# Gate/up with the activations stationary and 512 moving weight columns, x turned before it is normalised, two layers unrolled

## What is computed

```python
D_MODEL, SEQ, DEPTH, D_FF = 1024, 256, 2, 2816

def rms_norm(x, g):
    y = x * rsqrt(mean(x * x, -1) + 1e-6)
    return y * g

def swiglu_ffn(x, w_gate, w_up, w_down):
    return (silu(x @ w_gate) * (x @ w_up)) @ w_down

x = x + 0.5 * swiglu_ffn(rms_norm(x, ffn_norm), w_gate, w_up, w_down)
```

## Time and profile before

| | |
|---|---|
| median of 3 runs | 1089.12 us (1088.06 to 1089.48) |
| profiled execution, from its first to its last instruction | 1087.3 us; it is the time of that execution that the profile gives |
| TensorE busy | 1053.6 us (97%) |
| VectorE busy | 587.2 us (54%) |
| ScalarE busy | 493.3 us (45%) |
| GpSimd busy | 103.5 us (10%) |
| mean rate from memory | 164 GB/s |

### The profile page before, as it was taken

One profiled execution on the slowest core, in us unless ns is written; L12 is line 12 of the kernel. 1 busy time (PEld: TensorE's weight loads), 2 busy tenths in 40 slices (PEclk: granted clock), 3 DMA queues, 4 the chain that ended last, 5 costly groups with the idle time before them and its releaser, 6 DMA issues.

```text
span 1087.3 us, 18211 instructions
## 1 busy us (share of the span) xinstructions
PE 1053.6 (97%) x7148; PEld 949.8 (87%) x7148; DVE 587.2 (54%) x630; ACT 493.3 (45%) x656; POOL 103.5 (10%) x165
## 2 busy tenths in 40 slices
PE   6999999999989999999989999999998999999996
PEld 6999999778768999999889999998796789999995
DVE  4644454755665654445465544457456655445544
ACT  6443344447434544443364344335555354433342
POOL 2000000330341000000010000005004210000000
PEclk9999999999979999999999999999999899999999
DMA  9565455253212455545545555554252126554551
GB/s 327 197 219 186 182 190 193 80 192 140 106 56 88 158 191 193 193 169 182 191 166 197 191 193 187 181 173 148 99 181 78 39 79 232 187 183 174 190 204 48
DMA packets 26277, 178.38 MB, mean 164 GB/s; under 512 B 3152, under 2 KB 3664, under 8 KB 5360
## 3 DMA queue, kind: packets, MB, share of 16 engines
q1 hardware_dynamic: 24912, 174.73, 44.3%
q0 software_dynamic: 880, 2.74, 0.8%
q10 hardware_dynamic: 432, 0.18, 0.1%
HBM read 176.94 MB, written 1.05 MB: 164 GB/s over the span
## 4 chain that ended last, share of the span: by engine, by line
PE 63%; issue 28%; POOL 5%; ACT 1%; DVE 1%; DMA 1%; POOLq 0%; DVEq 0%; SPq 0%; ACTq 0%
PE psum L882 20%; PE psum L883 20%; PE psum L884 20%; POOL mixer_scratch L306 3%; PE psum L1103 1%; PE psum L899 1%; DMA w_raw<-in_w_dram 1%; PE psum L972 1%; ACT w_high L367 1%; POOL statistics L283 1%; POOL mixer_scratch L333 0%; POOL mixer_scratch L338 0%; POOL statistics L293 0%; ACT mixer_scratch L438 0%; PE psum L967 0%
## 5 line engine op out<-in xcount | busy, mean ns | idle before, releaser
L588 DVE TENSOR_TENSOR w_low<-w_raw,w_high 128x2048 fp32r<-128x2048 f32 x163 | 375.3, 2305 | 245.7 <-ACT w_high L367 245.7
L882 PE MATMUL psum<-xT_high,w_high 128*128 128x256 f32 x1536 | 436.1, 284 | 5.4 <-DVE xT_low L593 4.5
L883 PE MATMUL psum<-xT_low,w_high 128*128 128x256 f32 x1536 | 434.6, 283 | 0.0
L884 PE MATMUL psum<-xT_high,w_low 128*128 128x256 f32 x1536 | 434.6, 283 | 0.0
L367 ACT ACTIVATE w_high<-w_raw 128x2048 fp32r<-128x2048 f32 x163 | 311.1, 1914 | 124.9 <-PE psum L884 119.9
L882 PEld LDWEIGHTS psum<-xT_high,w_high 128*128 128x128 f32 x1536 | 294.6, 192 | 8.9 <-DVE xT_low L593 5.3
L883 PEld LDWEIGHTS psum<-xT_low,w_high 128*128 128x128 f32 x1536 | 294.6, 192 | 1.5
L884 PEld LDWEIGHTS psum<-xT_high,w_low 128*128 128x128 f32 x1536 | 294.6, 192 | 0.0
L396 ACT ACTIVATE silu_gate<-psum 128x256 f32<-128x256 f32 x88 | 33.7, 383 | 273.1 <-PE psum L884 273.1
L882 PE MATMUL psum<-w_high,hT_high 128*128 128x512 f32 (+1 forms) x360 | 139.9, 389 | 0.0
L883 PE MATMUL psum<-w_low,hT_high 128*128 128x512 f32 (+1 forms) x360 | 139.7, 388 | 0.0
(11 more groups left out here) (163 smaller groups left out, 804.9 us busy)
## 6 DMA issues: line engine op xcount, KB each, us to landing
w_raw<-in_w_dram SPq DMA_DIRECT2D x163, 1024.0 KB, 4.8
x<-in_x_dram SPq DMA_DIRECT2D x2, 512.0 KB, 4.3
mixer_scratch<-in_fil_dram POOLq DMA_DIRECT2D x2, 512.0 KB, 6.8
out_dram<-x_normed SPq DMA_DIRECT2D x4, 256.0 KB, 2.1
mixer_scratch<-in_fil_dram POOLq DMA_DIRECT2D x2, 384.0 KB, 7.4
mixer_scratch<-in_fil_dram POOLq DMA_DIRECT2D x2, 352.0 KB, 5.9
dft<-in_dft_dram SPq DMA_DIRECT2D x1, 512.0 KB, 6.8
inverse_dft<-in_dft_dram SPq DMA_DIRECT2D x1, 512.0 KB, 6.5
```

Source lines behind the costliest of these rows:

```text
L588: e.tensor_tensor(WL[p][:], raw[p][:], WH[p][:].bitcast(F32), ALU.subtract).then_inc(s_lo.sem, 1)
L882: e.matmul(out, ah, bh, start=start, stop=False)
L883: e.matmul(out, ah, bl, start=False, stop=False)
L884: return e.matmul(out, al, bh, start=False, stop=stop)
```

## The change

It does these things:

- Gate/up has x stationary and the weights moving. A slot now holds four of the eight inner tiles with 256 gate and 256 up columns side by side, so each of 48 matmuls per chunk has 512 moving columns. The product is tokens x hidden units: one PSUM bank per token tile (4 and 5), no second set.
- Since down needs hidden units x tokens, TensorE transposes the 128 x 128 blocks of `hidden` in float32 (`turn_hidden`, four per chunk, into bank 6), and `ht_high` and `ht_low` read that bank.
- Before an FFN x is transposed as it is (`turn_x`), partly between the last matmuls of the stage before; rstd enters as the scale of silu and as a factor in `gate`. Before the mixer, VectorE writes x times rstd (`normed`), and TensorE transposes that. No diagonal, no product with it.
- GpSimd multiplies rstd by sqrt(1024) in a fourth step.
- The loop over the layers is unrolled; linked waits are on constants. The spare fetch at the end goes.
- At stage ends two slots' splits, not one, are made before the updates.

```diff
+XT_BANKS = [(7, 6), (0, 1)]
+HT_BANK = 6
...
-            def x_rstd(l, j, link=link):
+            def x_rstd(l, j):
...
-                    e.tensor_tensor(r, r, cst[:, I_POW:I_POW + 1], ALU.pow).then_inc(s_rstd.sem, 1)
+                    link(e.tensor_tensor(r, r, cst[:, I_POW:I_POW + 1], ALU.pow))
+                    e.tensor_tensor(r, r, cst[:, I_SD:I_SD + 1], ALU.mult).then_inc(s_rstd.sem, 1)
...
+            def x_high(l, turn, t, half, col):
+
+                g = 2 * t + half
+                e.wait_ge(s_tr.sem, s_tr.at(l, 4 * turn + g + 1))
+                for n in range(4):
+                    k = 4 * half + n
+                    r = e.activation(XH[:, k, t * P:(t + 1) * P], PS[:, XT_BANKS[t][half], n * P:(n + 1) * P], ACT.Copy,
+                                     scale=par[:, col + k:col + k + 1])
+                r.then_inc(s_xh.sem, 1)
+
+            def enter(l, j, turn, col):
+
+                e.wait_ge(s_par.sem, s_par.at(l))
+                x_high(l, turn, 0, 0, col)
+                x_high(l, turn, 0, 1, col)
+                squares(l, j, (0,))
+                x_high(l, turn, 1, 0, col)
+                x_high(l, turn, 1, 1, col)
+                squares(l, j, (1,))
...
+                e.activation(sg[:, t, :], PS[:, 4 + t, 0:SEQ], ACT.Silu, scale=st[:, T_R + t:T_R + t + 1]).then_inc(s_silu.sem, 1)
...
+            def ffn(l, f, base, j, turn, col, after):
+                if l or f:
+                    enter(l, j, turn, col)
+                for t in range(T):
+                    e.wait_ge(s_rstd.sem, s_rstd.at(l, 2 * j + t + 1))
+                hi(l, base + 2)
+                hi(l, base + 3)
+                for t in range(T):
+                    silu(l, j, f * CH, t, base + 1)
+                ht_high(l, f * CH, 0, 0)
+                hi(l, base + 4)
 
                 def chunk(c, pr):
 
+                    q = f * CH + c
+                    ht_high(l, q - 1, 1, 1 - pr)
+                    hi(l, base + 3 * c + 2, (pos(base + 2), base // RING + c + 1))
+                    for t in range(T):
+                        silu(l, j, q, t, base + 3 * c)
+                    ht_high(l, q, 0, pr)
+                    hi(l, base + 3 * c + 3, (pos(base), base // RING + c + 2))
+                    hi(l, base + 3 * c + 4, (pos(base + 1), base // RING + c + 2))
...
-            squares(0, 0)
-            hi(0, 0)
             e.wait_ge(s_par0.sem, 16)
             e.sem_inc(s_par.sem, 1)
-            with e.Fori(0, DEPTH) as l:
+            enter(0, 0, 0, C_G1)
+            hi(0, 0)
+            hi(0, 1)
+            for l in range(DEPTH):
...
+            def normed(l, j, t):
 
                 e.wait_ge(s_rstd.sem, s_rstd.at(l, 2 * j + t + 1))
+                e.tensor_scalar(xn[:, t, :], x[:, t, :], st[:, T_R + t:T_R + t + 1], None, ALU.mult).then_inc(s_xn.sem, 1)
...
+            def gate(l, q, t):
+                e.wait_ge(s_silu.sem, s_silu.at(l, 2 * q + t + 1))
+                e.scalar_tensor_tensor(out=hid[:, t, :], in0=PS[:, 4 + t, SEQ:2 * SEQ], scalar=st[:, T_R + t:T_R + t + 1], in1=sg[:, t, :],
+                                       op0=ALU.mult, op1=ALU.mult).then_inc(s_h.sem, 1)
...
+            def update_and_enter(l, slot, scale, j, at, turn, col):
+
+                update(l, slot, scale, j, 0, 0)
+                update(l, slot, scale, j, 0, 1)
+                x_low(at, turn, 0, 0, col)
+                update(l, slot, scale, j, 1, 0)
+                x_low(at, turn, 0, 1, col)
+                update(l, slot, scale, j, 1, 1)
+                x_low(at, turn, 1, 0, col)
+                x_low(at, turn, 1, 1, col)
...
+            def ffn(l, f, base, after):
+                lo(l, base + 2)
+                lo(l, base + 3)
+                for t in range(T):
+                    gate(l, f * CH, t)
+                ht_low(l, f * CH, 0, 0)
+                lo(l, base + 4)
                 if f == 0:
                     argument(l, 0, 7, C_FB1, C_FF1)
...
+                    ht_low(l, q - 1, 1, 1 - pr)
+                    lo(l, base + 3 * c + 2, pos(base + 2))
+                    for t in range(T):
+                        gate(l, q, t)
+                    ht_low(l, q, 0, pr)
+                    lo(l, base + 3 * c + 3, pos(base))
+                    lo(l, base + 3 * c + 4, pos(base + 1))
...
                 lo(l, FFN2)
-                update(l, S_WO + 3, 1.0, 1)
-                ffn(l, 1, FFN2, 2, 3, C_G2)
+                lo(l, FFN2 + 1)
+                update_and_enter(l, S_WO + 3, 1.0, 1, l, 3, C_G2)
...
+            def turn_x(l, j, t, half):
+
+                e.wait_ge(s_x.sem, s_x.at(l, 4 * j + 2 * t + half + 1))
+                for n in range(4):
+                    k = 4 * half + n
+                    r = e.transpose(PS[:, XT_BANKS[t][half], n * P:(n + 1) * P], x[:, t, k * P:(k + 1) * P], ident)
+                r.then_inc(s_tr.sem, 1)
...
+            def gate_up(l, turn, n, p, half, tiles, fresh=False):
+
+                for t in tiles:
+                    for kk in range(4):
+                        k = half * 4 + kk
+                        if fresh and kk == 0:
+                            e.wait_ge(s_xl.sem, s_xl.at(l, 4 * turn + 2 * t + half + 1))
+                        r = passes(PS[:, 4 + t, :], XH[:, k, t * P:(t + 1) * P], XL[:, k, t * P:(t + 1) * P], WH[p][:, kk, :], WL[p][:, kk, :],
+                                   k == 0, k == KD - 1)
+                    if half and t == 0:
+                        r.then_inc(s_gu.sem, 1)
+                    if t == 1:
+                        r.then_inc(s_used.sem, 1)
+
+            def turn_hidden(l, q, t):
+
+                e.wait_ge(s_h.sem, s_h.at(l, 2 * q + t + 1))
+                for h in range(2):
+                    r = e.transpose(PS[:, HT_BANK, h * SEQ + t * P:h * SEQ + (t + 1) * P], hid[:, t, h * P:(h + 1) * P], ident)
+                r.then_inc(s_ht.sem, 1)
...
+                e.wait_ge(s_lo.sem, s_lo.at(l, base + 1))
+                gate_up(l, turn, base, pos(base), 0, (0,), True)
+                if l or f:
+                    turn_x(l, j, 1, 0)
+                    turn_x(l, j, 1, 1)
+                e.wait_ge(s_lo.sem, s_lo.at(l, base + 2))
+                gate_up(l, turn, base + 1, pos(base + 1), 1, (0,), True)
+                gate_up(l, turn, base, pos(base), 0, (1,), True)
+                gate_up(l, turn, base + 1, pos(base + 1), 1, (1,), True)
+                if f == 0:
+                    filter_mm(l, 0, F_W1, fil[:, F_Z:F_Z + SEQ], HYE, 7)
+                turn_hidden(l, f * CH, 0)
...
+                    e.wait_ge(s_lo.sem, s_lo.at(l, base + 3 * c))
+                    e.wait_ge(s_h.sem, s_h.at(l, 2 * q))
+                    gate_up(l, turn, base + 3 * c - 1, pos(base + 2), 0, range(T))
+                    e.wait_ge(s_hl.sem, s_hl.at(l, 2 * q - 1))
+                    turn_hidden(l, q - 1, 1)
+                    e.wait_ge(s_lo.sem, s_lo.at(l, base + 3 * c + 1))
+                    gate_up(l, turn, base + 3 * c, pos(base), 1, range(T))
+                    e.wait_ge(s_hl.sem, s_hl.at(l, 2 * q))
+                    turn_hidden(l, q, 0)
...
+                    down(l, base + 3 * c + 1, pos(base + 1), q - 1, 1 - pr, first)
```

More of the change, by code:

```diff
@@ L659, in ffn @@
                     chunk(i * 2 + 3, 1)
-                chunk(CH - 1, (CH - 1) % 2)
                 q, pr = f * CH + CH - 1, (CH - 1) % 2
-                gate(l, q, 0, pr)
+                ht_low(l, q - 1, 1, 1 - pr)
                 lo(l, base + FFN_SLOTS - 1)
+                for t in range(T):
+                    gate(l, q, t)
                 ht_low(l, q, 0, pr)
-                gate(l, q, 1, pr)
+                if after is not None:
+                    lo(l, after)
                 ht_low(l, q, 1, pr)
@@ L1064, in project @@
                 return r
-            with e.Fori(0, DEPTH) as l:
-                ffn(l, 0, 0, 0, 0)
+            e.wait_ge(s_cst.sem, 16)
+            for t in range(T):
+                turn_x(0, 0, t, 0)
+                turn_x(0, 0, t, 1)
+            for l in range(DEPTH):
+                ffn(l, 0, 0, 0, 0, None)
                 e.wait_ge(s_in.sem, 16 * N_IN)
@@ L1235, in ffn_slots @@
         at = slice(c * 256, (c + 1) * 256)
+        both = np.concatenate([gate[:, at], up[:, at]], 1).reshape(2, 4, P, 512)
         for half in range(2):
-            r = slice(at.start + half * P, at.start + (half + 1) * P)
-            a = np.stack([gate[:, r].reshape(KD, P, P), up[:, r].reshape(KD, P, P)], 2)
-            out.append(a.transpose(1, 0, 2, 3).reshape(P, SLOT))
+            out.append(both[half].transpose(1, 0, 2).reshape(P, SLOT))
         if last is not None:
```

319 lines of the change are left out of this document (154 added, 165 removed).

## The result

The changed kernel takes **1103.18 us** (1101.95 to 1105.51, 4 runs) against 1089.03: **1.0135** times the time before, 95% interval 1.0122 to 1.0148. It is slower, where 1092.7 (1079 to 1100) was forecast. The profiled execution took 1102.18, its span is 1100.3 us, 13.0 more than before.

The account below looks back on a forecast made before the run. TensorE, busy 1053.6 of 1087.3 us, was taken as the bound: its instructions' start-to-start distances plus gaps between stages. Terms summed to +3.6, 1087.3 to 1090.9 in span, forecast as 1092.7 us, range 1079 to 1100.

Parts of the forecast that it names:

- The clock: Half-clock falls behind new TensorE idles: 0 to 10 us; two places of 3.8 us idle counted, +4.
- Steady chunks: Gate/up in chunks 1 to 10 of four FFNs: wide matmuls gain 0.60, transposes take 0.44; 0.16 per chunk, 6.4 us less.
- The knife edge: Each steady chunk: new `hidden` is ready 0.1 us before its transposes; 0 taken, 0.3 per chunk (12 us) as bad end.
- Rival 3: Steady chunks: `hidden` late by 0.15 us in 40 chunks adds 6, giving 1099 us; chance 0.16.
- Rival 4: Gate/up: a wide matmul costs as much as two narrow steps, adding 26 us, giving 1119; chance 0.03.
- FFN 2's entry: Entry to FFN 2: gate/up starts 3.0 us earlier, but TensorE idles 3.8 before chunk 1; +0.8 each, +1.6.
- rival 1: Stage entries: `hidden` of chunk 0 ready when gate/up ends, so idles and clock falls go; 1081 us, chance 0.17.
- FFN 1 to mixer: Entry to the mixer, twice: x updates begin later behind a second w_low; 1.4 us later each, +2.8.
- Layer edge: Between the layers, once: jump and table load go, but updates wait for two w_low; -1.3 us.
- Start: Kernel start: ScalarE's x copies and squares precede the weight split, gate/up at 18.7 us, chunk 1 at 32.2; +4.5.
- Tail and unrolling: Output stored earlier at the end, -1.9 us; register instructions before linked waits go, mostly in the mixer, -0.6.
- Rival 2: Mixer keeps its clock because shorter POOL and VectorE links close the waits; 11 us less, 1082, chance 0.11.

Follow-up runs that it names:

- experiment 1: Changed kernel with filler transposes of the identity into a free bank in TensorE's idle places (start, mixer entries, before chunk 1); 1092.63 us, ratio 1.0025.
- narrow: Changed kernel with each gate/up matmul of 512 moving columns split into two of 256; 1126.53 us.
- twice_turned: Changed kernel with every pair of transposes of `hidden` issued twice into the same place; 1122.45 us.
- experiment 6: The run `narrow`: changed kernel with each gate/up matmul of 512 moving columns split into two of 256; 1126.53 us.
- experiment 9: Changed kernel with start, gate and updates reordered, tile-by-tile waits and the third slot's copy moved up; 1082.77 us, ratio 0.9930.
- experiment 4: Kernel before the change with only its loop over the two layers unrolled on every engine; 1085.48 us, ratio 0.9975.
- experiment 11: Kernel before the change with its layers unrolled and filler transposes in three waits of the mixer; 1082.84 us, ratio 0.9946.
- experiment 2: Changed kernel with the start reordered: squares first, then each x tile's copies alternating with a weight slot's; 1104.35 us, ratio 1.0129.
- combo2: The run of experiment 9: changed kernel with start, gate and updates reordered, tile-by-tile waits and the third slot's copy moved up; 1082.77 us, ratio 0.9930.
- combo3_fill: `combo2` plus filler (start, mixer), filter fetch ahead of the edge's rstd, both tiles multiplied with the first weight slot first; 1067.22 us, ratio 0.9807.
- experiment 5: Changed kernel with the second early w_low of each stage end put back behind the x updates; 1094.11 us, ratio 1.0043.
- experiment 3: Changed kernel with silu and gate product of chunk 0 ahead of the fourth slot's split, in all FFNs; 1095.49 us, ratio 1.0051.

## Why the prediction was wrong

The span came out 9.4 us above the forecast's 1090.9, and the range ended 3 us short. The queues were forecast rightly. The step that failed is the count of the clock's falls, which makes 3.1 of the 9.4. The others: some 2 in the chunks, 1.4 at the start, about 1 at the two mixer entries, and 0.9 because layer 2's mixer spent 13.7 us at half level and not 10.2, which is luck.

- **The clock: the step that failed.** "I count the two places of 3.8 us, +4." The same paragraph lists idles of 2.9 (twice) and 2.6, and at the start TensorE stands still for 10 us; none of these was counted. In the profiled execution all came: six stretches, not two. Filled, the six gave back 7.1 us (experiment 1), 3.1 more than the +4. The two that were counted cost 1.6 and 1.5 where 2 each was taken. The upper end of 10 us was in the text, but with it the sum is 1098.7, past the forecast's own 1096 and just inside the range; no room was left for the sum's other errors.
- **Steady chunks: right mechanism, too small a price.** -6.4 was forecast, 0.11 x 40 = 4.4 came (4.0 in the 36 of the table). The 0.11 for a transpose was the mean of four in a row with one slow step behind them; in a chunk there are two slow steps, so a pair is 0.27, not 0.22. The Trainium skill's rule for an isolated matmul (TensorE: Matmul & The Clock Gate, Back-to-back issue gap) gives one wide in place of two narrow ones 2.5 ns of gain, by which `narrow` would have cost 0.12 us a chunk; it cost 0.57. The same page's 275 ns for a bf16 transpose in a kernel (Part 4: PE-mode transpose), taken as a price, would have made `twice_turned` 1.1 us a chunk dearer; it was 0.41. In both the trace decides, for this kernel.
- **The knife edge held.** No pair of transposes waited in 40 chunks. Rival 3 is out. Rival 4 is out by experiment 6: two narrow ones cost 0.012 us more than a wide one.
- **FFN 2's entry: right.** Forecast were +0.8 and 2 for the clock, of which 1.6 and 1.5 came. The idle was 3.0 us (3.8), and from the first gate/up to chunk 1 it is 15.1 us (15.6). The cure stood in rival 1: its condition, `hidden` ready as gate/up ends, was a matter of order in two queues: with the order of experiment 9 TensorE waits nowhere there.
- **FFN 1 to mixer: the queue right, the clock missing.** The input projections start 2.3 us later, 1.4 of it forecast. The clock is 0.5 of the rest (experiment 1).
- **Layer edge.** -1.3 forecast, +0.9 came; the fall there is 1.6 (experiment 1), and what makes the rest is open. That unrolling makes the edge 1.3 us shorter is shown by experiment 4.
- **Start.** +4.5 forecast, +7.1 came. Gate/up at 19.33, not 18.7, since the parameters were there at 7.19, not 6.4; the slow clock is 1.4 more.
- **Tail and unrolling.** -1.9 forecast, -1.4 with the last pair of transposes; unrolling's -0.6 in the mixer is not to be seen.
- **Rival 2** had the waits as the cause of the mixer's fall, which experiment 11 bears out, but not its price: 11 us for both layers, where 3.3 + 2.4 = 5.7 are measured; and no link that the change shortens closes those waits.

## What to carry to other kernels

When a change makes idle places on TensorE, list them all and price each as its wait plus a stretch at half clock behind it, for waits of two or three microseconds too. The price of the stretch is set by the matmuls in it: 3.4 us cost 1.6 in dense gate/up and 0.5 at the mixer's entry. Filler that computes nothing, in a free bank, prices all this in one run, but compare place by place: part of what the total gains can be another stretch that came out shorter. In an engine with one queue, put what TensorE waits for ahead of what is needed only half a stage later: the same matmuls went from 1.35% slower to 0.4% faster than before by order alone. Price an instruction put into a dense stream by the whole stream up to where its steps are even again.

## What the hardware did that was not expected

- Neither whether a fall comes nor its length is given by the idle ahead of it. Behind the same 2.5 us at the mixer's entry the stretch was 3.4 us (changed kernel) and 13.7 (experiment 2). In the mixer it was 0 in layer 1 and 10.2 in layer 2 of one execution of `combo2`, with the same instructions and waits ahead; other runs have 3.4, 6.8 and 13.7. Behind 3.0 us at FFN 2's entry it was 3.4 or 6.8 us, or none (experiment 2, layer 2). This makes a kernel with such places scatter: 7 us over four runs of experiment 2, 2 us over five of `combo3_fill`.
- That idling brings the clock down and that the burst behind it then starts slow is what the Trainium skill says (TensorE: Matmul & The Clock Gate, HAM oscillation — how this bites in real kernels). The changed kernel's trace agrees at the five places where TensorE stood for 1.7 us or more between dense parts; behind 1.5 us, in layer 1's FFN 1, no fall came. Other traces set no bound there: experiment 5 has a fall behind the same 1.5 us, and experiment 2 none behind 3.0.
- Three waits of 1.2, 0.6 and 1.1 us within 9 us were enough in the mixer, though not each time (experiment 4). One of 0.8 between two dense parts was not (experiment 3), nor were 1.1 and 1.7 us within 4 us at the end of the mixer (experiment 11).
- The run with an edit of 5 us at the start differs most from some 180 us later on. That the edit moved it is not shown, since executions of one kernel differ as much. An edit is to be judged by its own stretch of the trace as well as by the total.
